# Two more projections of a two-block transformer kernel as block products, with GpSimd adding the squares of the norms behind them

## What is computed

```python
def short_conv_mixer(xn, w_in, conv_w, w_out):
    b, c, h = jnp.split(xn @ w_in, 3, axis=-1)
    u = causal_dwconv(c * h, conv_w)            # width 3
    return (b * u) @ w_out

def conv_ffn(xn, w_up, conv_w, w_down):         # 2816 hidden channels
    a, g = jnp.split(xn @ w_up, 2, axis=-1)
    return (jax.nn.silu(causal_dwconv(a, conv_w)) * g) @ w_down

x = x + short_conv_mixer(rmsnorm_2(x, attn_norm[0]), ...)
x = x + conv_ffn(rmsnorm_2(x, ffn_norm[0]), ...)
h = rmsnorm_2(x, kv_norm); kvf = h @ w_kvf      # and so on
```

## Time and profile before

| what | value |
|---|---|
| median of 3 runs | 2006.23 us (2005.51 to 2006.6) |
| the profiled execution's own time | 2005.84 us |
| its span, first to last instruction | 2004.1 us |
| PE busy | 1996.7 us, 100% of the span |
| DVE, ACT, POOL busy | 1200.4, 902.4, 900.7 us |
| DMA, mean | 96 GB/s |
| TensorE clock granted | 1.0 throughout |

### The profile page before, as it was taken

One profiled execution on the slowest core, in us unless ns is written; L12 is line 12 of the kernel. 1 busy time (PEld: TensorE's weight loads), 2 busy tenths in 40 slices (PEclk: granted clock), 3 DMA queues, 4 the chain that ended last, 5 costly groups with the idle time before them and its releaser, 6 DMA issues.

```text
span 2004.1 us, 28874 instructions
## 1 busy us (share of the span) xinstructions
PE 1996.7 (100%) x11386; PEld 1690.9 (84%) x11386; DVE 1200.4 (60%) x1985; ACT 902.4 (45%) x1389; POOL 900.7 (45%) x388
## 2 busy tenths in 40 slices
PE   9999999999999999999999999999999999999999
PEld 7888888888989898888888989888877778898988
DVE  4688878734747454434557557444367755755757
ACT  6445556534535434512434334246367743433423
POOL 4344444644545444444445445443422234544544
PEclk9999999999999999999999999999999999999999
DMA  5222222443333233322322333233321123233322
GB/s 181 79 91 74 85 85 74 127 140 95 105 97 113 86 106 95 105 92 88 105 95 95 105 95 110 88 97 95 95 64 53 53 85 95 95 106 95 113 85 98
DMA packets 55286, 192.49 MB, mean 96 GB/s; under 512 B 6128, under 2 KB 6640, under 8 KB 55152
## 3 DMA queue, kind: packets, MB, share of 16 engines
q1 hardware_dynamic: 55152, 190.65, 29.9%
HBM read 188.53 MB, written 2.10 MB: 95 GB/s over the span
## 4 chain that ended last, share of the span: by engine, by line
PE 97%; DVE 1%; DMA 1%; issue 0%; SPq 0%; ACT 0%; DVEq 0%; ACTq 0%
PE ps L1887 25%; PE ps L1889 25%; PE ps L1888 25%; PE ps L1909 5%; PE ps L1910 5%; PE ps L1911 5%; PE ps L2318 1%; PE ps L2284 1%; PE ps L2309 1%; PE ps L2243 1%; PE ps L2242 1%; PE ps L2241 1%; DMA w_raw<-in_panels 1%; PE ps L2085 1%; PE ps L1953 0%; PE ps L1983 0%
## 5 line engine op out<-in xcount | busy, mean ns | idle before, releaser
L440 POOL TENSOR_TENSOR w_lo<-w_raw,w_hi 128x1024 fp32r<-128x1024 f32 (+1 forms) x353 | 860.8, 2443 | 1026.3 <-ACT w_hi L485 990.9
L1887 PE MATMUL ps<-a_hi,w_hi 128*128 128x512 f32 x1152 | 456.6, 396 | 0.2 <-DVE x L1272 0.2
L1889 PE MATMUL ps<-a_hi,w_lo 128*128 128x512 f32 x1152 | 449.1, 390 | 0.0
L1888 PE MATMUL ps<-a_lo,w_hi 128*128 128x512 f32 x1152 | 448.9, 390 | 0.0
L485 ACT CAST w_hi<-w_raw 128x1024 fp32r<-128x1024 f32 (+1 forms) x353 | 362.0, 1033 | 130.2 <-PE ps L1889 45.9
L1887 PE MATMUL ps<-b_hi,w_hi 128*128 128x512 f32 x1000 | 390.1, 390 | 0.2 <-DVE x L1272 0.2
L1889 PE MATMUL ps<-b_hi,w_lo 128*128 128x512 f32 x1000 | 389.2, 389 | 0.0
L1888 PE MATMUL ps<-b_lo,w_hi 128*128 128x512 f32 x1000 | 389.1, 389 | 0.0
L1044 DVE TENSOR_TENSOR arena<-ps,inv_rms 128x512 f32<-128x512 f32 x176 | 121.2, 689 | 310.2 <-PE ps L1889 292.6
L1887 PEld LDWEIGHTS ps<-a_hi,w_hi 128*128 128x128 f32 x1152 | 216.3, 188 | 47.7 <-issue 2.7
L1888 PEld LDWEIGHTS ps<-a_lo,w_hi 128*128 128x128 f32 x1152 | 216.4, 188 | 45.9 <-issue 2.2
(11 more groups left out here) (277 smaller groups left out, 3151.5 us busy)
## 6 DMA issues: line engine op xcount, KB each, us to landing
w_raw<-in_panels SPq DMA_DIRECT2D x337, 512.0 KB, 3.6
w_raw<-in_panels SPq DMA_DIRECT2D x16, 384.0 KB, 3.2
x<-in_xT SPq DMA_DIRECT2D x16, 256.0 KB, 2.7
outT<-x SPq DMA_DIRECT2D x7, 256.0 KB, 3.1
consts<-in_const SPq DMA_DIRECT2D x1, 528.5 KB, 7.8
arena<-in_rows SPq DMA_DIRECT2D x1, 256.0 KB, 5.0
arena<-in_ws SPq DMA_DIRECT2D x1, 256.0 KB, 5.3
outT<-x SPq DMA_DIRECT2D x2, 128.0 KB, 1.8
```

The lines of the kernel that those rows point to most:

```text
L440: nc.gpsimd.tensor_tensor(w_lo[:, p % RING, 0:n], w_raw[:, p % RING, 0:n], w_hi[:, p % RING, 0:n].bitcast(F), ALU.subtract).then_inc(w_low, 1)
L1887: nc.tensor.matmul(o, wh, hi[:, kt, :], start=(kt == 0), stop=False)
L1888: nc.tensor.matmul(o, wh, lo[:, kt, :], start=False, stop=False)
L1889: ins = nc.tensor.matmul(o, wl, hi[:, kt, :], start=False, stop=(kt == tiles - 1))
```

## The change

- out2 becomes a folded stage of eight hidden tiles, the six-tile projection of the first conv ffn a folded stage of six.
- In conv_ch the two scaled panels go to other buffers, the hidden tile goes to the buffers of the folded stages, and DVE, ACT and POOL make its parts in the tail of each tile as in a folded ffn.
- Inside the two new folded stages DVE makes `low_x` for two tiles per pair, behind `add_crossing` of the pair after theirs (behind `add_third` at the end); ACT squares and splits two tiles per pair, behind its second `high`; POOL adds the squares (seven adds of 128x512 per norm), placed behind `low` of the sixth, eighth and tenth panel from the stage's start. DVE adds no squares there.
- Panels, their sizes and the DMAs stay; no load is added or taken away.

```diff
-FOLDED = [("ff1", 0), ..., ("ff1", 2)] + [(f"ffn_{_l}", _n) ... if (_l, _n) != (0, 2)]
+FOLDED = [("ff1", 0), ..., ("ff1", 2)] + [("out2", 0)] + [(f"ffn_{_l}", _n) for _l in range(2) for _n in range(3)]
+TOTALLED = [("out2", 0), ("ffn_0", 2)]
...
@@ gpsimd
+            def sum_squares(s, m):
+                pool.wait_ge(squared, 8 * s + m + 1)
+                if m == 0:
+                    return
+                if m > 1:
+                    pool.wait_ge(summed, 8 * s + m)
+                of = squares[:, 0, :] if m == 1 else sum_sq[:, :]
+                nc.gpsimd.tensor_tensor(sum_sq[:, :], of, squares[:, m % 2, :], ALU.add).then_inc(summed, 2 if m == 1 else 1)
+            def totals_behind(p):
+                for key in TOTALLED:
+                    p0, tiles = down_stage(*key)
+                    tiles_at = {p0 + 5: (0, 1), p0 + 7: (2, 3), p0 + 9: (4, 5, 6, 7)}
+                    for m in tiles_at.get(p, ()):
+                        sum_squares(TOTAL_OF[key], m)
             for p in range(N_PANELS):
                 low(p)
+                totals_behind(p)
                 low_t23_behind(p)
@@ scalar, down_pairs
                     high(p + FEED + 1)
+                    if j > 0 and key in TOTALLED:
+                        square_and_split(key, 2 * j - 2)
+                        square_and_split(key, 2 * j - 1)
                     if more:
                         for i in range(3):
                             high_of_sum(PAIR_AT[p + 2], i, tiles // 2 * P)
+                if key in TOTALLED:
+                    square_and_split(key, DT - 2)
+                    square_and_split(key, DT - 1)
+                    split_total(TOTAL_OF[key])
+            def square_and_split(key, m):
+                act.wait_ge(evicted, down_stage(*key)[0] + m + 1)
+                square_x(TOTAL_OF[key], m)
+                split_x(m, NORM_OF[key][1], B)
@@ scalar, conv_ch
                 high(p + FEED)
                 high(p + FEED + 1)
+                if m == DT - 1:
+                    high_of_sum(PAIR_AT[p + 2], 0, h)
+                    high_of_sum(PAIR_AT[p + 2], 1, h)
                 act.wait_ge(hid_raw, m + (8 * FF1_CHUNKS + 1))
-                split(a_hi[:, m, :], conv_o[:, m % 2, :]).then_inc(hid_high, 1)
-            residual(S["out2"], S_FFN0, "ffn_0", B)
-            split_total(S_FFN0)
+                high_tile(key, m, keep[m] if m < DT // 2 else hidden(m), a_hi)
...
+                    high_sums(key, m, a_hi)
+                if m == DT - 2:
+                    copy_a21(PAIR_AT[p + 4], DT)
+            down_pairs(("out2", 0))
@@ vector, down_pairs
                         add_crossing(p0, j)
+                        if key in TOTALLED:
+                            low_pair(key, 2 * j - 2)
                         continue
...
                 add_third(p0, DT // 2 - 1)
+                if key in TOTALLED:
+                    low_pair(key, DT - 2)
+                    rest_of_total(TOTAL_OF[key])
@@ vector, conv_ch
-                scale_out(conv_c[:, j, :], p).then_inc(evicted, 1)
-                scale_out(conv_t[:, j, :], p + 1).then_inc(evicted, 1)
+                scale_out(conv_t[:, j, :], p).then_inc(evicted, 1)
+                if m == DT - 1:
+                    sum_rest(PAIR_AT[p + 2], DT)
+                scale_out(padded[:, j, 2:SEQ + 2], p + 1).then_inc(evicted, 1)
                 dve.wait_ge(evicted, p + 2)
-                link(v.tensor_tensor(padded[:, j, 2:SEQ + 2], conv_c[:, j, :], conv_t[:, j, :], ALU.mult))
+                link(v.tensor_tensor(padded[:, j, 2:SEQ + 2], padded[:, j, 2:SEQ + 2], conv_t[:, j, :], ALU.mult))
...
+                if m < k2:
+                    low_first(key, m, A)
+                    t1(key, m)
+                    low_t1(key, m, A)
+                elif m < DT - 1:
+                    t2_t3(key, m - k2, k2)
+                    low_rest(key, m - k2, A, k2)
+                    t4(key, m - k2, k2)
+                    low_t4(key, m - k2, k2)
+                    if m == DT - 2:
+                        sum_first(PAIR_AT[p + 4], DT)
+                        sum_third(PAIR_AT[p + 4], DT)
+                else:
+                    low_of_sum(PAIR_AT[p + 2], 0, DT)
+                    last_tile(key, A)
+            down_pairs(("out2", 0))
@@ tensor
-            for part in ((0, 7), (7, DT)):
-                for m in range(2):
-                    product(S["out2"] + m, a_hi, a_lo, DT, hid_low, HID_CONV, part)
-            linear(S["out2"] + 2, DT - 2, a_hi, a_lo, None, None)
+            down_pairs(("out2", 0), A)
```

More of the change, by code:

```diff
@@ L48 @@
 HALF = SEQ // 2
-FOLDED = [("ff1", 0), ("ff1", 1), ("ff1", 2)] + [(f"ffn_{_l}", _n) for _l in range(2) for _n in range(3) if (_l, _n) != (0, 2)]
+FOLDED = [("ff1", 0), ("ff1", 1), ("ff1", 2)] + [("out2", 0)] + [(f"ffn_{_l}", _n) for _l in range(2) for _n in range(3)]
+TOTALLED = [("out2", 0), ("ffn_0", 2)]
 def down_stage(name, n):
@@ L55, in down_stage @@
         return START["ff1"] + 16 * n + DT, DT
+    if name == "out2":
+        return START["out2"], DT
     return START[name] + 2 * sum(FF2_CHUNKS[:n + 1]) + DT * n, FF2_CHUNKS[n]
@@ L828, in _ @@
             for m in range(DT):
[L829 removed]
+                p, key, h = S["conv_ch"] + 2 * m, ("out2", 0), DT // 2 * P
                 high(p + FEED)
                 high(p + FEED + 1)
+                if m == DT - 1:
+                    high_of_sum(PAIR_AT[p + 2], 0, h)
+                    high_of_sum(PAIR_AT[p + 2], 1, h)
                 act.wait_ge(hid_raw, m + (8 * FF1_CHUNKS + 1))
[L833 to L835 removed]
+                high_tile(key, m, keep[m] if m < DT // 2 else hidden(m), a_hi)
+                if m == DT - 1:
+                    high_of_sum(PAIR_AT[p + 2], 2, h)
+                    high_t23(key, m)
+                    high(p + 2 + FEED)
+                    copy_a21(PAIR_AT[p + 2] + 1, DT)
+                    high_t4(key, m)
+                else:
[3 more added lines that the diff above has]
+            down_pairs(("out2", 0))
             def ffn(l):
@@ L877, in ffn @@
                     t0 += size
-                    if key in FOLDED:
-                        down_pairs(key)
-                    elif n == len(FF2_CHUNKS) - 1 and l == 0:
-                        residual(p0, S_ATTN1, "kv", B)
-                        split_total(S_ATTN1)
-                    else:
-                        for m in range(DT):
-                            high(p0 + m + FEED)
+                    down_pairs(key)
                     p0 += DT
@@ L1260, in down_pairs, with low_pair @@
                     add_crossing(p0, j)
+                    if key in TOTALLED:
+                        low_pair(key, 2 * j - 2)
                 add_third(p0, DT // 2 - 1)
+                if key in TOTALLED:
+                    low_pair(key, DT - 2)
+                    rest_of_total(TOTAL_OF[key])
+            def low_pair(key, m0):
+                n, name = NORM_OF[key]
+                for m in range(m0, m0 + 2):
+                    low_x(n, m, name, B)
             def rest_of_total(s):
@@ L1710, in ffn @@
                     t0 += size
-                    if key in FOLDED:
-                        down_pairs(key)
-                        p0 += DT
-                        continue
-                    last = n == len(FF2_CHUNKS) - 1
-                    if last and l == 0:
-                        residual(p0, S_ATTN1, X_KV, "kv", B)
-                        rest_of_total(S_ATTN1)
-                    else:
-                        for m in range(DT):
-                            wait_made(p0 + m)
-                            if p0 + m < N_PANELS - 1:
-                                v.tensor_tensor(x[:, m, :], x[:, m, :], bank(p0 + m), ALU.add).then_inc(evicted, 1)
-                                continue
-                            for part in range(2):
-                                at = slice(part * SEQ // 2, (part + 1) * SEQ // 2)
-                                v.tensor_tensor(x[:, m, at], x[:, m, at], bank(p0 + m)[:, at], ALU.add).then_inc(evicted, 1)
+                    down_pairs(key)
                     p0 += DT
```

13 lines of the change are left out of this document (7 added, 6 removed).

## The result

The changed kernel takes **2015.61 us** (median of 6 runs, 2014.45 to 2017.06), beside 2006.26 for the kernel before (6 runs, 2005.51 to 2006.6). The ratio is 1.0048, 95% interval 1.0037 to 1.0058: slower by 9.4 us. The forecast was 2013.0 with 2005.0 to 2016.5 around it.

The account below looks back on a forecast made before the run. The matrix engine, busy for the whole span, was taken as the bound. out2's terms sum to +2.45 us and the six-tile stage's to +4.8, together +7.2 on 2005.84: 2013.0 us, range 2005.0 to 2016.5.

Parts of the forecast that it names:

- What bounds the kernel: Whole kernel: the matrix engine is always busy, so time changes only by matmul work removed or idle time appearing there.
- Work removed, out2 -4.0: out2's products: 44.00 us becomes the 39.99 of an already folded stage of eight hidden tiles, -4.0 us.
- The late last tile, 3.75: out2's first pair: conv_ch's last hidden tile comes late, so the pair ends 3.75 us late, DVE winning at tile 6.
- rival 3: Worse ties: GpSimd's queued instruction always goes first, out2's first pair ends 6.0 late, total 2015.2 us; chance 0.10.
- Side adds, 0.25: out2's second pair: side adds of the first pair hold its block two by 0.25 us.
- The fourth pair, 1.9: out2's fourth pair: one `low_x` waits for a GpSimd `low`, the first add is late, PE waits 1.9 us.
- The end of out2, 0.55: Behind out2: GpSimd's sums alternate with the last four `low_x`, tile 7 is split late for the next stage, 0.55 us.
- Six tiles, -0.6 + 0.8 + 3.4: Six-tile stage: -0.6 us of products, +0.8 from a longer loop in the third pair, +3.4 of PE waiting in the fourth.
- The end, 1.2: Behind the six-tile stage: the same alternation of sums and `low_x`, tile 7 ready at 5.9 against 4.76, 1.2 us.
- The norm's GpSimd adds: Norm behind out2's pairs: seven adds per norm at 1.30 us each, two per pair, cost nothing by themselves.
- 1 (the meetings miss): DVE's two-SBUF instructions don't run into GpSimd's, `low_x` costs 0.75 us each, total 2005.5 us, no change; chance 0.23.
- 2 (the columns decide): DVE's slack takes `low_x` and the late tile, the stages keep -4.0 and -0.6, total 2001.2 us; chance 0.07.

Follow-up runs that it names:

- the run with out2 alone: Changed kernel with only out2 folded and its norm behind it, the six-tile projection plain as in the kernel before: 2010.46 us, ratio 1.0023 to the kernel before.
- the run with PSUM: Full change, with conv_ch's first scaled panel and convolution kept in PSUM: 2011.4 us, ratio 1.0027 to the kernel before.
- the mended version: Only out2 folded, plus five edits to conv_ch's scaling and split order and to the norm's sums and low parts: 2003.93 us, ratio 0.9989 to the kernel before.

## Why the prediction was right, and where its terms were off

The direction, the places and the mechanism held; the time was 2.6 us short (2013.0 for 2015.61), of which 1.0 is the sum and the rest mostly the clock. That the sum missed by so little is in part luck: the late last tile was 2.5 too cheap, while the end of out2, the six tiles, the last end and the side adds were 0.55, 0.8, 0.2 and 0.15 too dear. By its own steps:

- **What bounds the kernel**: held. Every difference is a wait of PE, or its clock.
- **Work removed, out2 -4.0**: held. A pair that nothing holds takes 10.00, four would be 40.
- **The late last tile, 3.75**: mis-sized by the tie. conv_ch +2.92 and the first pair +3.34 at clock 1.00 make 6.26 in the run with out2 alone. The step that failed is the sentence that lets DVE win at tile 6. With GpSimd first it says 6.0, which is rival 3, given 0.10. Without the lock the prediction has 2.05; taking the multiply out of the lock's reach left 1.0 + 1.8.
- **Side adds, 0.25**: 0.1 in the run with out2 alone, where the second pair is 10.10.
- **The fourth pair, 1.9**: held, 2.15 and 1.97; one `low_x` gets through and the other takes 2.88.
- **The end of out2, 0.55**: 0 (7.23 for 7.25). The sums had begun earlier and the last `low_x` were not late. It became real only when GpSimd's work was held back: 1.1.
- **Six tiles, -0.6 + 0.8 + 3.4**: +2.83 for +3.6. The pairs were 8.35, 7.94, 8.45 and 10.73 where 8.8 and about 11 were named for the last two. The end, 1.2: 1.02.
- **The norm's GpSimd adds "nothing by themselves"**: with 1.3 us each, as taken, they took 1.29 and no wait of PE in the first three pairs of either stage leads to them. In the fourth pairs and behind them they are part of the meetings, as the prediction has it at the end.
- **Reading of the rows**: for VectorE beside GpSimd with an operand in PSUM the prediction cites 0.68 us in the earlier trace rows, but that add ends at 1244.77, before the `low` of 1244.85. The one beside it is the add of 0.41 at 1245.88, as short as others of its size, and the multiply of 0.69 in the run with PSUM shows the same. The 0.34% beside the sum should be 0.36%.
- **Not in the sum**: the fall of the granted clock, about 1.4 us in the profiled execution. The two executions of the changed kernel with a mean clock of 1.000 took 2014.45 and 2014.66, the four below it 2015.19 to 2017.06.

With the measured terms the sum at full clock is -4.0 + 6.26 + 0.1 + 2.0 + 2.83 + 1.0 = +8.2, so 2014.0 on the profiled execution before, and 1.4 more where the clock falls: 2015.4.

Of the rivals: 1 (the meetings miss) is out, since every meeting named is in the trace. 3 was true at the tie of tile 6, but not always: in the fourth pair `low_x`, waiting since 995.44, went ahead of the `low` of 995.87. Its total of 2015.2 is nearest to the result, though partly by chance, since six tiles came cheaper and the clock dearer. The rule of the Trainium skill that went with it (SBUF — State Buffer, "Who interferes with whom": "Issue order, not op shape, decides who blocks") fits this trace at both: `low` at 945.82 ahead of the multiply at 945.87, and `low_x` at 995.44 ahead of `low` at 995.87. 2 (the columns decide) named its point rightly, tile 7 ready before 3.93 us: even the mended version has it at 5.5 and gains 2.1 of the 4.0 in out2.

The condition that the prediction gave for the fourth pair also names what was mended: with the meeting and the alternation gone, the fourth pair is 10.00 and the seam 7.25.

## What to carry to other kernels

Before giving GpSimd or VectorE more two-SBUF work, lay both engines' instructions of one loop turn side by side: each such instruction on VectorE that can be put on a PSUM operand, or moved out of reach of a GpSimd pass, gave back up to 2.2 us on VectorE here (2.89 to 0.69), more than its own duration. Removed matmul columns pay only where the stage in front delivers its last tile in time and nothing is appended to the engine that paces the pair: out2 was worth 2.1 of 4.0 us after mending; the six-tile stage cost 2.9 us even then. When a wait is moved by a gate, look at the seam behind the stage and at the next consumer of each gated result: 1.1 of 1.95 us came back there.
